# A decoder block's expert stage: low parts of the weights written in place, eight ring slots, four high buffers

## The reference, cut to what matters

```python
gu = xb @ w_gate_up[e] + b_gate_up[e]          # 1024 x 2048
gate, up = jnp.split(gu, 2, axis=-1)
gate = jnp.minimum(gate, 7.0); up = jnp.clip(up, -7.0, 7.0)
act = (up + 1.0) * gate * jax.nn.sigmoid(1.702 * gate)
y = act @ w_down[e] + b_down[e]                # 1024 x 1024, times the token's share, added to its row
```

## Time and profile before

| | us |
|---|---|
| median of 3 runs | 1766.81 (1766.56 to 1767.76) |
| the profiled execution, own time | 1766.66 |
| its span | 1764.9 |
| TensorE busy | 1698.8 (96%) |
| VectorE busy | 1381.7 (78%) |
| ScalarE busy | 1200.8 (68%) |
| GpSimd busy | 713.1 (40%) |

### The profile page before, as it was taken

One profiled execution on the slowest core, in us unless ns is written; L12 is line 12 of the kernel. 1 busy time (PEld: TensorE's weight loads), 2 busy tenths in 40 slices (PEclk: granted clock), 3 DMA queues, 4 the chain that ended last, 5 costly groups with the idle time before them and its releaser, 6 DMA issues.

```text
span 1764.9 us, 24895 instructions
## 1 busy us (share of the span) xinstructions
PE 1698.8 (96%) x8477; PEld 1346.8 (76%) x8477; DVE 1381.7 (78%) x1048; ACT 1200.8 (68%) x967; POOL 713.1 (40%) x344
## 2 busy tenths in 40 slices
PE   6999999999999999999999999999999999999998
PEld 5878889777888987767767767767767767767776
DVE  4666776755334389999999999999999999999984
ACT  5565555433223368788788788788788788788775
POOL 6124233550000072355465365365365365365110
PEclk9999999999999999999999999999999999999999
DMA  5443343433336469999999999999999999999951
GB/s 177 122 129 85 121 122 107 121 108 119 96 96 231 164 218 397 391 404 392 399 402 392 399 401 392 402 406 388 404 404 391 405 400 398 402 400 395 408 201 49
DMA packets 150865, 504.64 MB, mean 286 GB/s; under 512 B 12733, under 2 KB 73285, under 8 KB 117173
## 3 DMA queue, kind: packets, MB, share of 16 engines
q1 hardware_dynamic: 141652, 478.49, 70.0%
q0 software_dynamic: 9104, 25.28, 6.0%
q10 hardware_dynamic: 48, 0.07, 0.0%
HBM read 487.63 MB, written 20.28 MB: 288 GB/s over the span
## 4 chain that ended last, share of the span: by engine, by line
PE 68%; DVE 14%; issue 9%; ACT 6%; POOL 2%; DVEq 0%; ACTq 0%; POOLq 0%
PE gu_ps L2395 13%; DVE split_l L1928 9%; PE gu_ps L2147 8%; PE gu_ps L2149 8%; PE gu_ps L2148 8%; PE dn_ps L2453 7%; PE gu_ps L2399 7%; PE dn_ps L2459 3%; ACT split_h L1303 3%; PE gu_ps L2409 2%; PE dn_ps L2652 1%; PE gu_ps L2652 1%; PE et_ps L2381 1%; DVE up_sb L1915 1%; PE gu_ps L2169 1%
## 5 line engine op out<-in xcount | busy, mean ns | idle before, releaser
L1928 DVE TENSOR_TENSOR split_l<-ring,split_h 128x2048 fp32r<-128x2048 f32 x384 | 864.8, 2285 | 71.0 <-ACT split_h L1303 69.3
L1303 ACT ACTIVATE split_h<-ring 128x2048 fp32r<-128x2048 f32 x384 | 729.9, 1913 | 113.8 <-PE gu_ps L2399 62.7
L914 POOL COPY icur<-slots 96x1 int32 x30 | 282.8, 9428 | 412.3 <-PE et_ps L2381 410.1
L1536 DVE TENSOR_TENSOR w_lo<-w_raw,w_hi 128x2048 fp32r<-128x2048 f32 (+1 forms) x45 | 104.3, 2318 | 128.8 <-ACT w_hi L1035 122.6
L2409 PE MATMUL gu_ps<-split_l,xgT_h 128*128 128x512 f32 x480 | 139.6, 412 | 17.8 <-DVE split_l L1928 14.0
L2147 PE MATMUL gu_ps<-hT_h,w_hi 128*128 128x512 f32 x392 | 154.6, 394 | 0.6 <-DVE acc L1589 0.6
L2149 PE MATMUL gu_ps<-hT_h,w_lo 128*128 128x512 f32 x392 | 152.7, 390 | 0.0
L2148 PE MATMUL gu_ps<-hT_l,w_hi 128*128 128x512 f32 x392 | 152.6, 389 | 0.0
L2395 PE MATMUL gu_ps<-split_h,xgT_h 128*128 128x512 f32 x512 | 140.6, 396 | 0.9 <-DVE xgT_l L1934 0.9
L2399 PE MATMUL gu_ps<-split_l,xgT_h 128*128 128x512 f32 x512 | 137.2, 390 | 0.0
L2395 PE MATMUL gu_ps<-split_h,xgT_l 128*128 128x512 f32 x512 | 137.2, 390 | 0.0
(11 more groups left out here) (426 smaller groups left out, 3242.1 us busy)
## 6 DMA issues: line engine op xcount, KB each, us to landing
ring<-in_w_gate_up SPq DMA_DIRECT2D x256, 1024.0 KB, 8.0
ring<-in_w_down SPq DMA_DIRECT2D x128, 1024.0 KB, 9.2
w_raw<-in_w_in SPq DMA_DIRECT2D x28, 1024.0 KB, 5.9
arow<-acum_rows POOLq DMA_DIRECT2D x16, 512.0 KB, 6.5
w_raw<-in_w_ssd_out SPq DMA_DIRECT2D x8, 1024.0 KB, 5.4
w_raw<-in_w_in SPq DMA_DIRECT2D x9, 512.0 KB, 6.1
w_raw<-in_w_mix_out SPq DMA_DIRECT2D x4, 1024.0 KB, 7.9
wpg<-in_w_ple_gate SPq DMA_DIRECT2D x2, 2048.0 KB, 19.9
```

The costliest lines, as they stand in the source:

```text
L914: g.tensor_copy(icur[:, :], col).then_inc(idx_done, 1)
L1303: a.activation(split_h[s % SPLIT][:, :], ring[s % RING][:, :], ACT.Copy).then_inc(hi_done, 1)
L1536: v.tensor_tensor(w_lo[RAW_SLOT[n]][:, 0:size], w_raw[RAW_SLOT[n]][:, 0:size], w_hi[HI_SLOT[n]][:, 0:size].bitcast(F32), ALU.subtract).the ...
L1928: v.tensor_tensor(split_l[s % SPLIT][:, :], ring[s % RING][:, :], split_h[s % SPLIT][:, :].bitcast(F32), ALU.subtract).then_inc(lo_done, 1)
```

## The change

Six things are changed.

1. `low` writes into the ring slot that it reads (`ring_low`, the same memory under the type fp32r). `split_l` is gone.
2. The ring has eight slots (two of them where `split_l` was), and `split_h` four buffers. `high` now waits for the chunk four places before to be used.
3. A load waits until TensorE has used the chunk eight places before it, no longer for the `low` of the chunk six places before. The seventh and eighth load of the stage wait for nothing.
4. On ScalarE and VectorE the split of chunk 12 stands ahead of the copy of the transposed rows, and that of chunk 16 ahead of the copy of the transposed activations; the evacuation of `dn_ps` on ScalarE stands one chunk later. Gate and clamp stay ahead of chunk 10's split.
5. POOL copies the token numbers one expert ahead, into `icur` and `icur_odd` in turn, so that the gather follows the transposes at once; the copy to `dcur` no longer waits for the result to be evacuated.
6. SP's loop goes over pairs of experts, since twelve chunks are no multiple of eight slots.

```diff
-RING = 6
-SPLIT = 3
+RING = 8
+FIRST = 6
+SPLIT = 4
...
             def gate_up(j, e, i, of, k, first=False):
-                slot = (UP + i) % RING
+                slot = slot_of(e, i)
                 if not first:
-                    sp.wait_ge(lo_done, chunk_at(j, e, i) + 1)
+                    sp.wait_ge(chunk_used, chunk_at(j, e, i) + CHUNKS - RING + 1)
...
-            for k in range(RING, UP):
-                gate_up(0, 0, k - UP, 0, k)
+            for k in range(FIRST, UP):
+                gate_up(0, 0, k - UP, 0, k, True)
...
+                def rows_ahead(e, rows_in, rows_out, index, other, more=True):
+                    pool.wait_ge(et_done, t0 + e * 2 + 4)
+                    alone(pool)
+                    pool.wait_ge(idx_done, k0 + e * 2 + 4)
+                    alone(pool)
+                    fetch(rows_in, index)
+                    if more:
+                        index_of(e + 4, other)
+                    scatter(e, slots[0:ROWS, column(e), 0], k0 + e * 2 + (6 if more else 5),
+                            slots[0:ROWS, column(e + 1), 1].bitcast(F32), True, rows_out, True)
...
                 def rest(e, more, rows_in, rows_act, folds=None):
-                    turned_high(t0 + 3 + e * 2, xgT_h, rows_in, 1.0 if more else 1.0 / ALPHA)
-                    for i in range(12, 14):
-                        high(j, e, i)
+                    high(j, e, 12)
+                    turned_high(t0 + 3 + n * 2, xgT_h, rows_in, 1.0 if more else 1.0 / ALPHA)
+                    high(j, e, 13)
+                    high(j, e, 14)
                     if folds is not None:
-                        half_down_out(e, e)
-                    high(j, e, 14)
+                        half_down_out(e, n)
+                    high(j, e, 15)
...
-                v.tensor_tensor(split_l[s % SPLIT][:, :], ring[s % RING][:, :], split_h[s % SPLIT][:, :].bitcast(F32),
-                                ALU.subtract).then_inc(lo_done, 1)
+                v.tensor_tensor(ring_low[slot_of(e, i)][:, :], ring[slot_of(e, i)][:, :],
+                                split_h[s % SPLIT][:, :].bitcast(F32), ALU.subtract).then_inc(lo_done, 1)
...
-                def rest(e, more, rows_act):
-                    for i in range(12, 16):
+                def rest(e, more, rows_act, rows_in):
+                    n = number(e)
+                    low(j, e, 12)
+                    if rows_in == HALF:
+                        turned_low(t0 + 3 + n * 2, xgT_h[:, :, HALF:P], xgT_h, HALF)
+                    else:
+                        turned_low(t0 + 3 + n * 2, xgT_l[:, :, 0:ROWS], xgT_h, ROWS, 1.0 if more else 1.0 / ALPHA)
+                    for i in range(13, 16):
                         low(j, e, i)
```

More of the change, by code:

```diff
@@ L364, in program @@
         top[0] = arena
-        ring = [here(f"ring{i}", [P, 2 * DM], F32) for i in range(RING)]
+        ring_off = top[0]
+        ring = [here(f"ring{i}", [P, 2 * DM], F32) for i in range(FIRST)]
+        top[0] = ring_off
+        ring_low = [here(f"ring_low{i}", [P, 2 * DM], F32R) for i in range(FIRST)]
         xg_off = top[0]
@@ L374, in program @@
         split_h = [here(f"split_h{i}", [P, 2 * DM], F32R) for i in range(SPLIT)]
-        split_l = [here(f"split_l{i}", [P, 2 * DM], F32R) for i in range(SPLIT)]
+        ring_off = top[0]
+        ring += [here(f"ring{i}", [P, 2 * DM], F32) for i in range(FIRST, RING)]
+        top[0] = ring_off
+        ring_low += [here(f"ring_low{i}", [P, 2 * DM], F32R) for i in range(FIRST, RING)]
         xgT_off = top[0]
@@ L520, in program @@
         pen_done, last_idx = sem("pen_done"), sem("last_idx")
-        e_loaded = [sem(f"e_loaded{i}") for i in range(RING)]
+        e_loaded = [sem(f"e_loaded{i}") for i in range(FIRST)] + yT_loaded[0:RING - FIRST]
         hi_done, lo_done, et_hi = sem("hi_done"), sem("lo_done"), sem("et_hi")
@@ L729, in weights, with expert_loads @@
                     sp.wait_ge(order_done, 1)
-                with sp.Fori(1 if ahead else 0, NE - 1) as e:
-                    of, after = (position(sp, e), position(sp, e + 1)) if ahead else (e, e + 1)
-                    bias_parts(j * NE + e + 1, after)
+                def expert_loads(e):
+                    n = number(e)
+                    of, after = (position(sp, n), position(sp, n + 1)) if ahead else (n, n + 1)
+                    bias_parts(j * NE + n + 1, after)
                     for k in range(UP):
@@ L736, in weights @@
                         down(j, e, UP + r, of, r)
+                with sp.Fori(0, PAIRS) as i:
+                    for off in (1, 2) if ahead else (0, 1):
+                        expert_loads((i, off))
+                if not ahead:
+                    expert_loads(NE - 2)
                 of = position(sp, NE - 1) if ahead else NE - 1
@@ L748, in weights @@
                 alone(sp)
-            for k in range(RING):
+            for k in range(FIRST):
                 gate_up(0, 0, k - UP, 0, k, True)
@@ L2430, in half_down @@
                             o = t.matmul(dn_ps[:, b * 512:b * 512 + 512], actT_h[:, 2 * r + k, :],
[L2431 to L2432 removed]
+                                         part[:, k * DM + b * 512:k * DM + b * 512 + 512],
+                                         start=r == 0 and k == 0 and part is high_part, stop=False)
                 if r == DN - 1:
```

145 lines of the change are left out of this document (81 added, 64 removed).

## The result

The changed kernel takes 1783.84 us, the median of four runs (1780.79 to 1784.1), where the kernel before took 1767.03 in four (1766.56 to 1767.76): a ratio of 1.0093, interval 1.0080 to 1.0105. That is 16.8 us slower. 1758.7 was forecast, with a range of 1744 to 1773: the sign was wrong, and the range did not hold the time. The profiled execution took 1783.77 us, with a span of 1782.0.

The account below looks back on a forecast made before the run. It took VectorE to pace half chunks and TensorE full ones; 0.75 us per pair over 15 pairs plus 1.3 made 12.6 us, cut to 8 for loads: 1766.7 - 8 = 1758.7 us, range 1744 to 1773.

Parts of the forecast that it names:

- Gate, evacuation and chunk 12: Engine terms per expert pair: 0.9 us gained at the gate, 0.4 by moved ScalarE copies, 0.55 lost; net 0.75 gained.
- The move behind chunk 12: Rows' low-part copy behind chunk 12's split, at the border to a full gate_up: 0.55 us lost per pair.
- the wait for `xgT_l`: Sign at the border to a full gate_up: TensorE waits about 0.5 us for the rows' low parts.
- the other border: Start of the half gate_up: the rows' low part comes later, but TensorE runs into the join as before; nothing lost.
- What earlier loads are worth: Expert-stage loads: whether DMA engines have room to keep up decides the gain, from 0 to all; two thirds, 8 us, taken.
- the 12.6: Total gain in us if loads keep up: 11.3 over 15 pairs plus 1.3 at the last gate.
- Now the gather goes about 10 us earlier, away from the scatter ... so this is nothing by itself: GpSimd's loop: the gather moves about 10 us earlier, the scatter keeps its time; no effect on the total.
- Rival 1: Expert stage: transfers are the bound already, nothing gained; 1763.5 to 1768 us, middle 1766; chance 0.20.
- rival 3: Border to gate_up: the move behind chunk 12 outweighs the gains; 1778 us; chance 0.17, shared with the late-slot-freeing rival.
- Rivals 1, 3 and 4: Transfers already bound (0.20); chunk 12's move outweighs gains, or slots freed later starve loads, 1770 us and up (together 0.17).
- The last gate: End of the expert stage: the last gate, with no full gate_up behind it, gains another 1.3 us.
- TensorE never waited for xg: Gathered rows: TensorE had no waits for them, so an earlier gather was taken to be worth nothing by itself.

Follow-up runs that it names:

- e5: The kernel before the change, with only the second half of each expert chunk loaded (wrong weights): ratio 1.0000 to the kernel before, period 65.79 us.
- e4: The changed kernel with only the second half of each expert chunk loaded (wrong weights): ratio 0.9938 to the kernel before, period 65.00 us.
- e11: The changed kernel with half of each load (wrong weights) and the rows' copies back ahead of chunk 12's split: ratio 0.9885 to the kernel before, period 64.37 us.
- e9: The changed kernel with the gather held until the result is evacuated, directly ahead of the scatter: ratio 1.0006 to the kernel before, period 65.83 us.
- e15: The changed kernel with the late gather, but the full expert's gather directly behind the scatter: ratio 1.0032 to the kernel before, period 65.75 us.
- e10: The changed kernel with the gather held until the scatter and the rows' copies ahead of chunk 12's split: ratio 1.0026 to the kernel before, period 66.15 us.
- e6: The changed kernel with each load held until both the new and the old slot rule allow it: ratio 1.0074 to the kernel before, period 66.67 us.
- e1: The changed kernel with GpSimd's old loop, the index copied in front of each gather: ratio 1.0092 to the kernel before, period 66.59 us.
- e3: The changed kernel with the rows' copies again ahead of chunk 12's split, all loads whole: ratio 1.0038 to the kernel before, period 66.23 us.
- e12: The changed kernel with the rows' copies ahead of chunk 12's split and GpSimd's old loop: ratio 1.0058 to the kernel before, period 66.21 us.
- e2: The kernel before the change with GpSimd's new loop alone: ratio 1.0003 to the kernel before, period 65.83 us.

## Why the prediction was wrong

**Gate, evacuation and chunk 12 (right).** 0.75 us per pair was the sum; 65.79 - 65.00 = 0.79 was measured with the transfers away (e5, e4). The clamp stands 0.08 us from the gate (0.2 forecast) and the next subtraction 2.86 us behind the gate (2.9). The move behind chunk 12 was 0.55 and is 0.63 (e11); the wait for `xgT_l` is 8.4 / 15 = 0.56 us where loads keep up (0.5 forecast). At the other border, where "nothing" was forecast, TensorE waits 13.3 / 14 = 0.95 us, with half loads too; since both borders together cost 0.63, hardly any of it is left at the end of the pair.

**"What earlier loads are worth" (the step that failed).** "I take 8 us, two thirds, since ten waits in 360 chunks are nearer to 'they keep up'." They don't, and nothing is had of the 12.6: with half of each load the engines take 65.00 us per pair, with whole loads 66.72. Few waits said only that the transfers were done in the period of before; they said nothing of a shorter one. e9 and e15, which wait 45.1 and 36.5 us for loads, move the same bytes in 65.83 and 65.75 us: in these orders too the transfers give no more than the period of before. The share of 1.01 hinted at it. The rate of 426 GB/s in the earlier trace rows was read as room; it was taken between the scatter and the next gather, and these come in every pair. The 435 GB/s of the Trainium skill (DMA: Bandwidth & Descriptors, Specifications) are not reached over a pair by any kernel here: over twelve pairs 399 is the highest with all bytes moved, over a single pair 408 (e10). The argument that a slot freed 1.6 us earlier lets a load start earlier was right and brought nothing that e6 could measure.

**"Now the gather goes about 10 us earlier, away from the scatter ... so this is nothing by itself" (wrong in the price).** The full expert's gather did go 10.8 us earlier, as forecast; the half expert's ends 2.0 us later than before, since the wait went into its own instruction. The scatter did not keep its time: it came 6.5 us earlier, less than the gather. Once the transfers are the bound this has a price: 66.72 against 65.83 us for the same bytes (e9), which is all of the loss in the period. This is the part that no rival had: transfers that are not only the bound but slower than before. Why they are slower with the gather in that place is not shown, nor whether its distance from the scatter or its own moment in the pair counts. e1 is no witness against it: with the old loop and 66.59 us it too has this gather 7.2 us ahead of the scatter.

**Rival 1** (the transfers are the bound) is what the kernel met, **rival 3** how it then lost: VectorE comes to chunk 12 late because ScalarE waits for loads, and the border is paid. Its sign, a wait for `xgT_l` of 1.3 us, is there with 19.7 / 15 = 1.31. The later start of the half `gate_up` (13.3 us) is there too, but it is no sign of late loads, since e4 has the same. Its 1778 was 11 us for this; the twelve periods and the last pair cost 12.4. But its mechanism alone does not explain the sum: e9 has the wait for `xgT_l` too (15.9 us) and loses nothing in the period. Rivals 1, 3 and 4 together had been given 0.37.

**The last gate** was to bring 1.3 us; the end of the stage costs 3.8. TensorE's wait behind ScalarE's standstill is 1.8 of it, the stretch at half the clock about 1.6 and the border 0.65; the sum had none of the three there. "TensorE never waited for xg" held for after, not for e3, e10 and e12.

**What stays open:** why a gather at another moment makes 26 MB take 0.9 us longer; what ScalarE stands still for at the end of the stage; and where the 0.3% between e15 and e9 lie. No version here is faster than the kernel before with all its work done. e11 shows what waits behind the bound: 64.37 us per pair, 1.1% of the time. e10 reaches that period in single pairs with all its bytes; which order of gathers and scatters would hold it is not shown.

## What to carry to other kernels

When the DMA share is full in every stretch and three engines stand within 7% of the period, first ask for the transfers' own period: run the kernel with half of each load, and then the faster engines with all of it; a few waits for loads don't tell how far away that bound is. Earlier issue of the loads brought nothing here, where the queue was never empty (e6). When a small copy on GpSimd takes 10 us beside a busy VectorE, look whether it is a wait: here it moved to the next instruction when the copy went (e2). When an edit moves an indirect DMA, look up in the trace where it really went, for each place in the loop by itself.

## What the runs showed of the hardware that was not expected

A DMA share of 1.01 is no proof of a bound: halving the bytes of all loads left the time of the kernel before at 1.0000, with a share of 0.66. Nor does it say how fast the bytes go: with a share of 1.01 or 1.02 the same bytes moved at 394 or at 399 GB/s over twelve pairs, by the place of one indirect DMA, and at 408 over one pair of e10. GpSimd's copy of 96 numbers took 9.7 us at one place of the pair before and 24.3 there in e12; at the other place it took 10.3 before and 0.8 in e12. And a wait of TensorE of 1.5 us at the end of the stage was followed by 3.4 us at half the granted clock.
